# A two-block transformer on one core: GpSimd's weighing by a spread tensor, PE's first late sum moved, another order at the ends of two layers, a store in four parts

## The chip, the cores and the metric

The kernel runs on one core of one Trainium2 chip. The metric is the device time of one execution in microseconds (us). Engines are called PE (TensorE, matmuls), DVE (VectorE), ACT (ScalarE), POOL (GpSimd) and SP (SyncE, which only issues DMAs here).

## The reference

One sequence of 256 tokens with 1024 channels goes through two blocks of two layers each. All of it is in float32.

```python
def first_block(x, c, ...):
    for l in range(2):
        mod = silu(c) @ ada_w[l] + ada_b[l]
        sh_m, sc_m, gt_m, sh_f, sc_f, gt_f = split(mod, 6)
        h = rms_norm(x, norm_mix) * (1 + sc_m) + sh_m
        o_a, o_b, o_c = banded, sparse and delta mixers of split(h @ w_in)
        x = x + gt_m * (concat(o_a, o_b, o_c) @ w_out)
        h = rms_norm(x, norm_ffn) * (1 + sc_f) + sh_f
        gate, up = split(h @ w_gate_up)
        x = x + gt_f * ((silu(gate) * up) @ w_down)
    return rms_norm(x, final_norm)

def second_block(x, ...):
    for layer in range(2):
        h = rmsnorm(x, attn_norm[layer])
        mixed = 16 heads of biased attention on split(h @ w_in)   # even and odd layer differ
        x = x + mixed @ w_o[layer]
        h = rmsnorm(x, ffn_norm[layer])
        x = x + conv_ffn(h, w_up[layer], ..., w_down[layer])
    return rmsnorm(x, final_norm)
```

The change touches how a part of `silu(c) @ ada_w` is summed (a vector of 1024 times a matrix of 1024x512 for each of 24 chunks of the modulation), the order of work in `mixed @ w_o` of the even and the odd layer, and the store of the result.

## The kernel before, in words

Activations lie transposed: `x`, `h` and `mix` are [128 partitions, 8 channel tiles, 256 tokens]. Each weight matrix streams from memory in chunks of 512 columns into a ring of three slots. A float32 product is made of three PE matmuls of rounded operands (lines 655 to 657): every half chunk is copied in rounded form by ACT (`high`, line 1445, tile w_hi), DVE subtracts that from the original (`low`, line 1961, tile w_lo, two inputs in SBUF), and PE multiplies high by high, high by low and low by high. The order of every engine's work is written out by hand in the program; semaphores join them.

Phases that matter here, in order: layer 0 and layer 1 of the first block each end with "gu" (11 gate chunks of four output tiles, loop `up` on PE, three chunks for each turn of a loop) and "dn" (8 down tiles, `down` on PE). The second block has an even and an odd layer; each ends with attention woven into the output projection.

**The late modulation sums.** Of the 24 chunks of `silu(c) @ ada_w`, 16 are multiplied on PE. The 8 others, numbers 10 to 15 in layer 0 and 22 and 23 in layer 1, are loaded by POOL itself while gu and dn run, in two halves of 4 row tiles each (`load_half`). POOL multiplies each row tile of 128x512 by its column of silu(c) (line 2644), and adds the 8 products to one row of 512 (lines 2646, 2649, 2651, 2652); that is `weigh`. PE then sums the row over partitions with four small matmuls (`modulations`, line 772), for which it waits on POOL in its own order: behind gate chunk 3 (the first of them), behind gate chunk 9 (the second), and in layer 0's dn ahead of down tiles 2, 3, 5 and 7 (the table NEXT_ADA and `next_modulation`). `late_sums` has two rows, so POOL's first add of chunk m waits until PE has summed chunk m-2 (the wait on mod_ready):

```python
pool.wait_ge(mod_ready, m - 1)
ch(G.tensor_tensor(out, ada_late[:, 0, :], ada_late[:, 1, :], ALU.add))
```

**The ends of the even and the odd layer.** Eight attention units (u0 to u0+7) each pass scores (PE, line 787), `logits` (DVE, lines 1990 to 1993), `exps` (ACT, line 1476), `recip` (DVE, line 2006), probabilities (POOL, line 2622), `transposes` (PE, line 799), `copy_pt` (ACT, line 1487), `values` (PE, line 812) and `evac` (DVE, line 2018, into mix). `mix_high_woven` (ACT, line 1737) and `mix_low_woven` (DVE, line 1973) split finished tiles of mix, at tiles 0 to 3, 4 and 5, and 6 and 7 (mix_ready +1, +2, +3). The output projection is written as `out_part(l, half, k0, k1, tiles)`: the product of half chunk `half` over mix tiles k0 to k1, three matmuls for each k and output tile, into the PSUM banks of OUT_BANKS. PE runs it in pieces between the last units. `residual` (DVE, line 2303) then adds the finished tiles to x in order and makes w_lo of three further half chunks between them, before the next norm.

**The end.** `normalise_into` (DVE, line 1926) writes the 8 tiles of h, and SP stores all of h with one DMA behind the last (line 621).

## Time and profile before

| what | value |
|---|---|
| median of three runs | 1637.39 us (1636.44 to 1639.26) |
| the profiled execution, whole | 1637.26 us |
| its span, first to last instruction | 1635.0 us |
| PE busy | 1508.4 us, 92% |
| DVE, ACT, POOL busy | 60%, 50%, 20% |
| mean granted PE clock | 0.962 |

The profiled execution is 0.13 us below the median and 2.26 us longer than its span. A busy PE is not a PE at its peak: a matmul of 256 columns is reported with 0.28 us, while in a dense stretch one starts every 0.12 us. So the views by time are of more use than the busy share: what PE waits for, and what lies in order of time around those waits.

### The profile page before, as it was taken

What the parts mean: (1) busy time and instruction counts of PE and PEld (TensorE: products, weight loads), DVE (VectorE), ACT (ScalarE), POOL (GpSimd) and SP (SyncE); (2) the same over time, 40 slices, a digit from 0 to 9 for tenths busy, and PEclk for the clock granted to TensorE, in tenths of its full rate; (3) what the DMA queues carried; (4) which work ended last, traced back from release to release, by engine and by line L of the source; (5) the groups of instructions that cost most, each with busy time, mean ns of one, the idle gap of its engine ahead of it and who ended that gap; (6) DMA issues with size and microseconds to landing.
All of it is one profiled execution on the core that took longest, in us unless ns stands there. A gap on an engine that the chain in (4) does not pass through costs nothing.

```text
span 1635.0 us, 29653 instructions
## 1 busy us (share of the span) xinstructions
PE 1508.4 (92%) x12380; PEld 1436.1 (88%) x12380; DVE 975.5 (60%) x1342; ACT 810.9 (50%) x1319; POOL 323.5 (20%) x174
## 2 busy tenths in 40 slices
PE   6989978899979899888999998889999999799997
PEld 3988868899979888788999998879999998799997
DVE  2675446465446764574545658657785645577854
ACT  3764355343326643553434444546664555466642
POOL 0002202999850022039200000100000001000000
PEclk8999999899989999998999999999999999999999
DMA  9435745564642465254445642343544643334442
GB/s 388 170 143 233 255 162 199 193 252 178 253 173 98 152 242 197 79 206 177 184 152 184 221 155 104 112 165 142 200 154 161 226 155 115 143 128 182 172 153 88
DMA packets 31493, 287.91 MB, mean 176 GB/s; under 512 B 3032, under 2 KB 11512, under 8 KB 11929
## 3 DMA queue, kind: packets, MB, share of 16 engines
q1 hardware_dynamic: 26968, 267.42, 44.3%
q0 software_dynamic: 2304, 16.78, 2.7%
q10 hardware_dynamic: 2112, 2.15, 0.4%
q8 instruction: 84, 1.38, 0.3%
q14 instruction: 25, 0.20, 0.0%
HBM read 285.23 MB, written 7.39 MB: 179 GB/s over the span
## 4 chain that ended last, share of the span: by engine, by line
PE 71%; DVE 8%; POOL 8%; ACT 6%; DMA 3%; issue 3%; SPq 0%; DVEq 0%; POOLq 0%; ACTq 0%
PE bank L655 20%; PE bank L656 20%; PE bank L657 20%; POOL arena L2644 4%; ACT w_hi L1445 2%; DMA ring<-w_out 2%; DVE w_lo L1961 2%; PE bank L968 1%; PE bank L799 1%; PE bank L758 1%; PE bank L812 1%; POOL arena L2646 1%; DVE h L1926 1%; PE bank L772 1%; PE bank L734 1%
## 5 line engine op out<-in xcount | busy, mean ns | idle before, releaser
L655 PE MATMUL bank<-hi_T,w_hi 128*128 128x256 f32 x2184 | 633.9, 290 | 30.7 <-DVE h_lo L1946 17.0
L657 PE MATMUL bank<-hi_T,w_lo 128*128 128x256 f32 x2184 | 627.5, 287 | 0.0
L1961 DVE TENSOR_TENSOR w_lo<-ring,w_hi 128x2048 fp32r<-128x2048 f32 (+1 forms) x226 | 481.4, 2138 | 190.5 <-ACT w_hi L1445 188.8
L656 PE MATMUL bank<-h_lo,w_hi 128*128 128x256 f32 x2056 | 591.5, 288 | 0.0
L1445 ACT ACTIVATE w_hi<-ring 128x2048 fp32r<-128x2048 f32 (+1 forms) x226 | 391.8, 1735 | 275.0 <-PE bank L657 252.6
L655 PEld LDWEIGHTS bank<-hi_T,w_hi 128*128 128x128 f32 x2184 | 430.0, 197 | 36.7 <-issue 29.7
L657 PEld LDWEIGHTS bank<-hi_T,w_lo 128*128 128x128 f32 x2184 | 429.3, 197 | 0.0
L656 PEld LDWEIGHTS bank<-h_lo,w_hi 128*128 128x128 f32 x2056 | 405.2, 197 | 0.5 <-issue 0.2
L655 PE MATMUL bank<-act_hi,w_hi 128*128 128x256 f32 x704 | 200.7, 285 | 0.7 <-DVE w_lo L1961 0.7
L656 PE MATMUL bank<-act_lo,w_hi 128*128 128x256 f32 x704 | 200.0, 284 | 0.0
L657 PE MATMUL bank<-act_hi,w_lo 128*128 128x256 f32 x704 | 200.0, 284 | 0.0
L2644 POOL TENSOR_SCALAR arena<-arena,c_silu 128x512 f32<-128x512 f32 x64 | 146.0, 2294 | 9.3 <-DMA arena<-ada 8.6
L2622 POOL TENSOR_TENSOR arena<-arena,rec 128x512 f32<-128x512 f32 (+1 forms) x16 | 25.8, 1611 | 586.8 <-DVE rec L2006 586.8
L655 PEld LDWEIGHTS bank<-act_hi,w_hi 128*128 128x128 f32 x704 | 136.1, 193 | 1.2 <-DVE w_lo L1961 1.2
L656 PEld LDWEIGHTS bank<-act_lo,w_hi 128*128 128x128 f32 x704 | 136.0, 193 | 0.0
L657 PEld LDWEIGHTS bank<-act_hi,w_lo 128*128 128x128 f32 x704 | 136.0, 193 | 0.0
L2586 DVE SCALAR_TENSOR_TENSOR arena<-bank,v,arena 128x254 f32<-128x254 f32 (+1 forms) x176 | 72.7, 476 | 37.6 <-ACT arena L1897 37.4
L656 PE MATMUL bank<-mix_lo,w_hi 128*128 128x256 f32 x256 | 74.2, 290 | 0.0
L655 PE MATMUL bank<-w_hi,hi_T 128*128 128x256 f32 (+2 forms) x240 | 69.8, 291 | 0.0
L656 PE MATMUL bank<-w_lo,hi_T 128*128 128x256 f32 (+2 forms) x240 | 68.6, 286 | 0.0
L657 PE MATMUL bank<-w_hi,h_lo 128*128 128x256 f32 (+2 forms) x240 | 68.6, 286 | 0.0
L1897 ACT ACTIVATE arena<-bank,v 128x256 f32<-128x256 f32 x88 | 44.7, 558 | 43.6 <-PE bank L657 43.6
(270 smaller groups left out, 1963.8 us busy)
## 6 DMA issues: line engine op xcount, KB each, us to landing
ring<-w_gu SPq DMA_DIRECT2D x22, 2048.0 KB, 7.7
ring<-w_dn SPq DMA_DIRECT2D x32, 1408.0 KB, 6.1
ring<-w_up SPq DMA_DIRECT2D x22, 2048.0 KB, 7.9
ring<-ada SPq DMA_DIRECT2D x16, 2048.0 KB, 9.0
ring<-w_mix SPq DMA_DIRECT2D x11, 2048.0 KB, 8.3
arena<-ada POOLq DMA_DIRECT2D x16, 1024.0 KB, 7.2
ring<-even_in SPq DMA_DIRECT2D x8, 2048.0 KB, 7.7
ring<-odd_in SPq DMA_DIRECT2D x6, 2048.0 KB, 7.9
```

Source lines behind the costliest of these rows:

```text
L655: nc.tensor.matmul(out, wh, xh, start=start, stop=False)
L656: nc.tensor.matmul(out, wh, xl, start=False, stop=False)
L657: return nc.tensor.matmul(out, wl, xh, start=False, stop=stop)
L734: last = nc.tensor.matmul(bank[:, 7, 0:S], const("ones"), h[:, k, :], start=(k == 0), stop=(k == KT - 1))
L758: last = nc.tensor.matmul(bank[rows, 7, 0:S], c_wide[:, k, :], w[:, k, half * S:half * S + S], start=k < 4, stop=k >= 4, tile_position=(0, ...
L772: last = nc.tensor.matmul(bank[:, 7, at:at + 1], sums_m[:, t * P:t * P + P], ones, start=True, stop=True)
L1445: nc.scalar.activation(w_hi[:, u % AHEAD, 0:size], ring[:, slot, part * size:(part + 1) * size], ACT.Copy)\
L1897: last = nc.scalar.activation(cv[:, b, half, :], bank[:, 2 * b + half, 0:S], ACT.Identity, bias=cb[:, at], scale=cw[:, 2, at])
L1961: V.tensor_tensor(w_lo[:, n % SLOTS, at], ring[:, n % SLOTS, at], w_hi[:, u % AHEAD, 0:size].bitcast(F32), ALU.subtract).then_inc(w_lo_rea ...
L2586: V.scalar_tensor_tensor(out=cv[:, b, half, shift:S], in0=bank[:, 2 * b + half, 0:S - shift], scalar=cw[:, tap, at], in1=cv[:, b, half, sh ...
L2622: ins = G.tensor_tensor(out, out, along(rec[:, b, :], w), ALU.mult)
L2644: ch.mark(G.tensor_scalar(ada_late[:, k, :], ada_late[:, k, :], c_silu[:, k:k + 1], None, ALU.mult))
```

## The change

Six edits. (1) GpSimd's multiplications are written as a product of two tensors, the second being one column of c_silu spread over the 512 elements; the adds of 128x1024 are replaced by adds of 128x512, so that a half has three or four adds in a row, all of them behind the wait on mod_ready in the first half. (2) PE does the first late sum of each gu phase behind the sixth gate chunk instead of behind the third. (3) Even layer: on PE the product for output tile 3 moves ahead of the last transposes, and that for output tile 5 ahead of the wait for the last mix tiles, for which it gets PSUM bank 4 instead of 0; on DVE the second split of mix moves ahead of the last logits. (4) Odd layer: on PE the first product for output tile 2 moves ahead of `values(u0 + 5)`, and on DVE `evac(u0 + 4)` ahead of the last `recip`. (5) An explicit wait on logits_done in the even layer. (6) The result is stored by four DMAs of two tiles each.

```diff
--- before.py
+++ after.py
@@ -505,7 +505,7 @@
         stage("odd", biased_units(0, 2, 0, 4, 1, 0, False, 4), lg_odd)
 
         WOVEN = (0, 1, 7)
-        OUT_BANKS = (0, 1, 7, 2, 3, 0, 1, 2)
+        OUT_BANKS = (0, 1, 7, 2, 3, 4, 1, 2)
         MIXED_BANKS = (4, 5, 6, 0, 2, 3, 1, 4)
 
         def evacs_before(u):
@@ -617,9 +617,10 @@
             load_phase("o1", w_o2[1], 0, full)
             load_phase("up1", w_up2[1], 4, full)
             load_phase("down1", w_dn2[1], 2, FT * P)
-            sp.wait_ge(h_ready, norm_end[-1])
-            sp.dma_start(y, h[:, :, :]).then_inc(y_out, 16)
-            sp.wait_ge(y_out, 16)
+            for k in range(0, KT, 2):
+                sp.wait_ge(h_ready, norm_end[-1] - KT + k + 2)
+                sp.dma_start(y[:, k:k + 2, :], h[:, k:k + 2, :]).then_inc(y_out, 16)
+            sp.wait_ge(y_out, 16 * KT // 2)
 
 
         @block.tensor
@@ -1055,9 +1056,9 @@
                             one(j, i * (2 * SLOTS) + u0 + 2 * j + 1, i * (4 * SLOTS) + t0 + 4 * j - 3)
 
                 if m_next:
-                    turn(0, 1)
+                    turn(0, 2)
                     modulations(m_next - 1, m_next)
-                    turn(1, turns)
+                    turn(2, turns)
                 else:
                     turn(0, turns)
                 for j in range(SLOTS * turns, 11):
@@ -1294,15 +1295,16 @@
                 out_part(0, 0, 4, 6)
                 out_part(0, 1, 4, 6, (0,))
                 values(u0 + 6)
+                pe.wait_ge(logits_done, u0 + 8)
+                out_part(0, 1, 0, 6, (1,))
                 transposes(u0 + 7)
-                out_part(0, 1, 0, 6, (1,))
                 out_part(0, 2, 0, 6, (0,))
                 values(u0 + 7)
+                out_part(0, 2, 0, 6, (1,))
                 pe.wait_ge(mix_ready, mixed + 3)
                 out_part(0, 0, 6, KT)
                 out_part(0, 1, 6, KT)
-                out_part(0, 2, 6, KT, (0,))
-                out_part(0, 2, 0, KT, (1,))
+                out_part(0, 2, 6, KT)
                 out_part(0, 3, 0, KT)
 
             def odd_layer(first):
@@ -1359,9 +1361,9 @@
                 pe.wait_ge(mix_ready, mixed + 1)
                 out_part(1, 0, 0, 4)
                 values(u0 + 4)
+                out_part(1, 1, 0, 4, (0,))
                 values(u0 + 5)
                 transposes(u0 + 6)
-                out_part(1, 1, 0, 4, (0,))
                 pe.wait_ge(logits_done, u0 + 8)
                 out_part(1, 1, 0, 4, (1,))
                 values(u0 + 6)
@@ -2501,8 +2503,8 @@
                 logits(u0 + 6)
                 recip(u0 + 6)
                 evac(u0 + 5)
+                mix_low_woven(mixed + 2, slice(4, 6))
                 logits(u0 + 7)
-                mix_low_woven(mixed + 2, slice(4, 6))
                 recip(u0 + 7)
                 evac(u0 + 6)
                 evac(u0 + 7)
@@ -2552,8 +2554,8 @@
                 low(h0 + 11 + AHEAD)
                 logits(u0 + 7)
                 recip(u0 + 6)
+                evac(u0 + 4)
                 recip(u0 + 7)
-                evac(u0 + 4)
                 evac(u0 + 5)
                 mix_low_woven(mixed + 2, slice(4, 6))
                 evac(u0 + 6)
@@ -2641,15 +2643,18 @@
                 out = late_sums[:, m % 2, :]
                 pool.wait_ge(late_in[half], 16 * (ada_alone.index(m) + 1))
                 for k in range(k0, k0 + KT // 2):
-                    ch.mark(G.tensor_scalar(ada_late[:, k, :], ada_late[:, k, :], c_silu[:, k:k + 1], None, ALU.mult))
+                    ch.mark(G.tensor_tensor(ada_late[:, k:k + 1, :], ada_late[:, k:k + 1, :],
+                                            along(c_silu[:, k:k + 1], CH), ALU.mult))
                 ch.wait()
-                ch(G.tensor_tensor(ada_late[:, k0:k0 + 2], ada_late[:, k0:k0 + 2], ada_late[:, k0 + 2:k0 + 4], ALU.add))
                 if half == 0:
                     pool.wait_ge(mod_ready, m - 1)
                     ch(G.tensor_tensor(out, ada_late[:, 0, :], ada_late[:, 1, :], ALU.add))
-                else:
-                    ch(G.tensor_tensor(out, out, ada_late[:, k0, :], ALU.add))
-                    G.tensor_tensor(out, out, ada_late[:, k0 + 1, :], ALU.add).then_inc(acc_ready, 1)
+                for k in range(max(k0, 2), k0 + KT // 2):
+                    last = G.tensor_tensor(out, out, ada_late[:, k, :], ALU.add)
+                    if k < KT - 1:
+                        ch(last)
+                if half:
+                    last.then_inc(acc_ready, 1)
                     pool.wait_ge(acc_ready, m + 1)
                 if m_next is not None:
                     load_half(m_next, half)
```

GpSimd's row of instructions for one late chunk. Before, ada_late lies in arena and late_sums in pT:

```order
26 L2644 TENSOR_SCALAR arena<-arena,c_silu 128x512 x3
27 L2646 TENSOR_TENSOR arena<-arena 128x1024 [waits pool_chain]
28 L2649 TENSOR_TENSOR pT<-arena 128x512 [waits mod_ready,pool_chain]
29 L2635 DMA arena<-ada 128x2048 [waits pool_chain]
30 L2644 TENSOR_SCALAR arena<-arena,c_silu 128x512 [waits late_in1]
31 L2644 TENSOR_SCALAR arena<-arena,c_silu 128x512 x3
32 L2646 TENSOR_TENSOR arena<-arena 128x1024 [waits pool_chain]
33 L2651 TENSOR_TENSOR pT<-pT,arena 128x512 [waits pool_chain]
34 L2652 TENSOR_TENSOR pT<-pT,arena 128x512 [waits pool_chain]
35 L2635 DMA arena<-ada 128x2048 [waits acc_ready]
```

And the same stretch of the changed kernel:

```order
26 L2646 TENSOR_TENSOR arena<-arena,c_silu 128x512 x3
27 L2651 TENSOR_TENSOR pT<-arena 128x512 [waits mod_ready,pool_chain]
28 L2653 TENSOR_TENSOR pT<-pT,arena 128x512 [waits pool_chain] x2
29 L2637 DMA arena<-ada 128x2048 [waits pool_chain]
30 L2646 TENSOR_TENSOR arena<-arena,c_silu 128x512 [waits late_in1]
31 L2646 TENSOR_TENSOR arena<-arena,c_silu 128x512 x3
32 L2653 TENSOR_TENSOR pT<-pT,arena 128x512 [waits pool_chain] x4
33 L2637 DMA arena<-ada 128x2048 [waits acc_ready]
```

One add of 128x1024 stood ahead of the wait on mod_ready; now all three adds of the first half stand behind it.

DVE at the end of the even layer, before (L2018 is evac of unit 5, L1990 to L1993 the logits of unit 7, L1973 the second split of mix):

```order
713 L2018 COPY mix<-bank 128x2x128 [waits pv_done]
714 L1990 SCALAR_TENSOR_TENSOR arena<-bank,small,arena 128x1024 [waits trans_ready,scores_ready]
715 L1992 TENSOR_TENSOR arena<-arena 128x1024 [waits dve_chain]
716 L1993 TENSOR_REDUCE negm<-arena 128x4 [waits dve_chain]
717 L1973 TENSOR_TENSOR mix_lo<-mix,mix_hi_woven 128x512 [waits mix_hi_ready]
718 L2006 RECIPROCAL rec<-sums 128x4 [waits exps_done]
```

And changed:

```order
713 L2020 COPY mix<-bank 128x2x128 [waits pv_done]
714 L1975 TENSOR_TENSOR mix_lo<-mix,mix_hi_woven 128x512 [waits mix_hi_ready]
715 L1992 SCALAR_TENSOR_TENSOR arena<-bank,small,arena 128x1024 [waits trans_ready,scores_ready]
716 L1994 TENSOR_TENSOR arena<-arena 128x1024 [waits dve_chain]
717 L1995 TENSOR_REDUCE negm<-arena 128x4 [waits dve_chain]
718 L2008 RECIPROCAL rec<-sums 128x4 [waits exps_done]
```

The split now precedes the logits of unit 7 and waits for ACT's copy.

DVE at the end of the odd layer, before (the two L2006 are units 6 and 7, the two L2018 units 4 and 5):

```order
966 L1993 TENSOR_REDUCE negm<-arena 128x4 [waits dve_chain]
967 L2006 RECIPROCAL rec<-sums 128x4 [waits exps_done] x2
968 L2018 COPY mix<-bank 128x2x128 [waits pv_done] x2
969 L1973 TENSOR_TENSOR mix_lo<-mix,mix_hi_woven 128x512 [waits mix_hi_ready]
970 L2018 COPY mix<-bank 128x2x128 [waits pv_done] x2
```

And changed:

```order
966 L1995 TENSOR_REDUCE negm<-arena 128x4 [waits dve_chain]
967 L2008 RECIPROCAL rec<-sums 128x4 [waits exps_done]
968 L2020 COPY mix<-bank 128x2x128 [waits pv_done]
969 L2008 RECIPROCAL rec<-sums 128x4 [waits exps_done]
970 L2020 COPY mix<-bank 128x2x128 [waits pv_done]
971 L1975 TENSOR_TENSOR mix_lo<-mix,mix_hi_woven 128x512 [waits mix_hi_ready]
```

The evac of unit 4 no longer stands behind the reciprocal of unit 7.

## Rows read from the trace of the kernel before

**Rows 1.** The page: the chain that ended last, by engine.

```profile
PE 71%; DVE 8%; POOL 8%; ACT 6%; DMA 3%; issue 3%; SPq 0%; DVEq 0%; POOLq 0%; ACTq 0%
```

**Rows 2.** Waits of PE: us in total, times, longest.

```profile
PE bank L772 <- POOL pT L2652: 23.4, 3, 8.7
...
PE bank L655 <- DVE mix_lo L1973: 4.8, 2, 2.8
```

**Rows 3.** PE in order of time, three late sums: start, us, ..., [idle before <-releaser].

```profile
310.53 1.87 PE L772 MATMUL bank<-cn,pT 128*128 128x1 f32 x8 [7.38 <-POOL pT L2652]
...
382.97 0.95 PE L772 MATMUL bank<-cn,pT 128*128 128x1 f32 x8
...
473.79 1.87 PE L772 MATMUL bank<-cn,pT 128*128 128x1 f32 x8 [8.66 <-POOL pT L2652]
```

**Rows 4.** Windows: stretch, length, PE busy (x), PEld, DVE, ACT, POOL, PEclk, DMA.

```profile
475.00:479.00 4.00, 4.00 (x20) 4.00 (x20) 0.34 (x2) 0.00 (x0) 0.00 (x0) 0.50 0.00 0
480.00:484.00 4.00, 4.00 (x36) 4.00 (x35) 0.00 (x0) 1.92 (x1) 0.00 (x0) 1.00 0.00 0
```

**Rows 5.** Groups of POOL by form: xcount, busy us, mean ns, idle before.

```profile
L2644 POOL TENSOR_SCALAR arena<-arena,c_silu 128x512 f32<-128x512 f32 x64 | 146.0, 2294 | 9.3 <-DMA arena<-ada 8.6
...
L2622 POOL TENSOR_TENSOR lg<-lg,rec 128x512 f32<-128x512 f32 x6 | 6.2, 1040 | 51.8 <-DVE rec L2009 30.0 <-DVE rec L2006 21.8
L2664 POOL TENSOR_TENSOR arena<-arena,v 128x1024 f32<-128x1024 f32 x2 | 5.7, 2870 | 247.0 <-ACT arena L1470 247.0
```

**Rows 6.** The line L2644, min/median/max ns of its instructions.

```profile
L2644 POOL TENSOR_SCALAR arena<-arena,c_silu x64: 1552/1570/4327, 276.5 to 775.4; 128x512 f32<-128x512 f32 x64
```

**Rows 7.** POOL in order of time: a multiplication, an add, two adds of dn.

```profile
278.10 3.23 POOL L2644 TENSOR_SCALAR arena<-arena,c_silu 128x512 f32<-128x512 f32 x1
286.43 2.41 POOL L2646 TENSOR_TENSOR arena<-arena 128x1024 f32<-128x1024 f32 x1
...
423.82 2.28 POOL L2649 TENSOR_TENSOR pT<-arena 128x512 f32<-128x512 f32 x1 [5.58 <-PE bank L772]
...
440.58 1.30 POOL L2652 TENSOR_TENSOR pT<-pT,arena 128x512 f32<-128x512 f32 x1
```

**Rows 8.** DVE in order of time, w_lo beside those POOL instructions.

```profile
277.61 2.29 DVE L1961 TENSOR_TENSOR w_lo<-ring,w_hi 128x2048 fp32r<-128x2048 f32 x1 [1.15 <-ACT w_hi L1445]
282.10 2.29 DVE L1961 TENSOR_TENSOR w_lo<-ring,w_hi 128x2048 fp32r<-128x2048 f32 x1 [1.42 <-ACT w_hi L1445]
...
287.86 3.13 DVE L1961 TENSOR_TENSOR w_lo<-ring,w_hi 128x2048 fp32r<-128x2048 f32 x1 [1.42 <-ACT w_hi L1445]
```

**Rows 9.** DVE by form in 423.8 to 473.8 us (layer 0's dn).

```profile
L1961 DVE TENSOR_TENSOR w_lo<-ring,w_hi 128x1408 fp32r<-128x1408 f32 x11 | 20.6, 1906 | 1.2 <-ACT w_hi L1445 1.2
```

**Rows 10.** Even layer in order of time, three engines.

```profile
1074.83 0.57 ACT L1487 ACTIVATE pT<-bank 128x512 f32<-128x512 f32 x1
...
1086.25 0.38 PE L655 MATMUL bank<-mix_hi_woven,w_hi 128*128 128x256 f32 x1 [1.91 <-DVE mix_lo L1973]
...
1090.47 2.29 DVE L1961 TENSOR_TENSOR w_lo<-ring,w_hi 128x2048 fp32r<-128x2048 f32 x1 [1.52 <-ACT w_hi L1445]
...
1100.53 0.41 DVE L2303 TENSOR_TENSOR x<-x,bank 128x256 f32<-128x256 f32 x1
```

**Rows 11.** Odd layer in order of time, three engines.

```profile
1397.14 1.44 PE L812 MATMUL bank<-pT,arena 128*64 128x128 f32 x16 [3.49 <-DVE mix L2018]
...
1396.51 0.18 DVE L2006 RECIPROCAL rec<-sums 128x4 f32<-128x4 f32 x1 [2.06 <-ACT arena L1476]
...
1412.56 1.92 ACT L1445 ACTIVATE w_hi<-ring 128x2048 fp32r<-128x2048 f32 x1 [2.69 <-PE bank L657]
```

**Rows 12.** DVE's last tiles; two DMAs of SP: KB each, us to landing.

```profile
1627.45 3.25 DVE L1926 SCALAR_TENSOR_TENSOR h<-x,cn,rstd 128x256 f32<-128x256 f32 x8
...
y<-h SPq DMA_DIRECT2D x1, 1024.0 KB, 3.9
...
c_in<-c SPq DMA_DIRECT2D x1, 4.0 KB, 1.6
```

## The prediction

> **What bounds the kernel now.** I read the chain of waits first. It gives PE 71% and POOL 8% of the span [rows 1]. POOL's 8% is no gain to be had: the chain follows POOL's work backwards while PE has work of its own beside it. What PE loses is in the list of its waits: 23.4 us in three stalls on line 772, the late modulation sums, all on POOL's last add, and 4.8 us in two stalls on a split of mix [rows 2]. In order of time the three are 7.38 us at 303 to 310 us (layer 0, behind gate chunk 3), the same in layer 1 (23.4 less the other two leaves 7.4), and 8.66 us at 465 to 474 us, the last late sum of layer 0's dn [rows 3]. A stall costs more than its length: the granted clock in the 4 us behind the third is 0.50, the lower of its two levels (1.2 GHz), and 1.00 in the next window, with 20 matmuls against 36 [rows 4]. Sixteen matmuls at 0.12 us are about 1.8 us.
>
> **Edit 2, the first late sum three chunks later.** PE fell idle at 303.2 (310.53 less 7.38) and reached the second sum at 382.97 [rows 3], 79.8 us later. Between lie six gate chunks of 96 matmuls, 69.1 us at 0.12 us. The sum itself stays and takes 0.8 us, as it does unheld (the row at 382.97 shows 0.95). The rest, 9.9 us, goes: PE asks at about 338, and POOL was done at 310.5. Layer 1 has the same stall, so 19.8 us together. What waits for that sum is POOL's first add of chunk 12, which it reaches at about 347.
>
> **Edit 1, GpSimd.** How long the new multiplication takes is not in the trace. The old one takes 1.55 us when nothing holds it (minimum, and the median 1.57) and 2.29 in the mean [rows 5, 6]. The nearest row is the probabilities of the same engine, 128x512 times a column spread over 128 elements: 1.04 us in the mean of six. Another spread product, the scaling of z, took 2.87 for 128x1024, or 1.43 for 512 [rows 5]. I take 1.04 and keep 1.43 for the range, and 1.55 as the far end. Adds take 1.30 for 512 and 2.4 for 1024 [rows 7], so a half of four multiplications saves 2.0 and pays 0.3 for its adds.
>
> The Trainium skill speaks against this edit: its page GPSIMD Engine Reference, section 3.1, gives an op of two inputs 2.6 cycles for each element and one of a single input 1.03, so a product of two tensors would be 2.5 times as long as the one it replaces. By an estimate from its figure, 512 elements at 1.2 GHz are 1.1 us, which agrees with the 1.04 of the row; its figure for one input, 0.44 us, doesn't agree with the 1.55 measured, and the measurement decides.
>
> The difference of 2.29 and 1.55 is DVE. A multiplication that began at 278.10 while DVE made w_lo (277.61 to 279.9) took 3.23 us, and the w_lo at 287.86 took 3.13 instead of 2.29 beside POOL's add of 286.43 to 288.84. But the w_lo at 282.10 took its 2.29 beside a multiplication [rows 7, 8]. So an instruction of two tensors on either engine holds up the other, and the old multiplication is held up without holding. The new one both is held and holds. I replayed layer 0 by this rule, with DVE's starts from the trace. With the old instructions it ends at 473.3, where the trace has 473.8 (the 473.79 of rows 3).
>
> Now the third stall. From the release by PE at 423.8 (where POOL had idled 5.58) [rows 7] POOL takes 50 us to 473.8: 12 multiplications at 1.55, three adds at 2.4, six at 1.3, two DMA issues at 0.95 and gaps, 36.3 us, and so 13.6 us held up. New: 12 at 1.04 and 14 adds at 1.30 (also the 2.4 us that stood ahead of the wait now stand behind it), with the rest 34.0 us. DVE makes 12 w_lo of about 1.6 us in that time [rows 9] (eleven, and the last of the size before them), 19.2 us. If these hold POOL up as much as before, the piece is 2.3 us shorter; if fully, 3.3 longer. The replay gives 50.4, so **0.5 us longer**. POOL must also come in time to that release, now about 413.8. By the replay it does, with 5.8 us to spare; at 1.30 for a multiplication it comes 7.3 late. What DVE loses is at most 1.3 us a w_lo. In gu that is nothing to PE, which has 5.8 us of matmuls in each half chunk and its w_lo two of them ahead. In dn the first w_lo of a pair has the 4.0 us (33 matmuls) of one half: 0.8 for the add before it, at most 1.3 held and 1.6 of its own are 3.7, just inside.
>
> **Edit 4, odd layer.** PE stalls 3.49 us on evac, which stood behind the reciprocal of unit 7 at 1396.51; without it, it can run at about 1394.5. From PE's idle at 1393.65 to ACT's next copy at 1412.56 [rows 11], which waits for the first two finished output tiles, are 18.9 us. The work between is 78 matmuls at 0.12 (9.4) and five groups of transposes and values (4.3) with 0.2 of latency: 13.9. Behind the move of 12 matmuls nothing else is late: POOL's last probabilities end at 1398.7, where PE arrives at 1398.7. So **5.0 us** go, which is the stall and 1.6 of the clock. Low end 3.5, the stall alone.
>
> **Edits 3 and 5, even layer.** The split comes about 2.9 us earlier and its stall goes. But unit 7's logits start 1.5 us later, and ACT copies unit 6's transposes (1074.83) only behind unit 7's exponentials. It does so at 1076.3 now, and PE, which reaches `values(u0 + 6)` at 1072.9, stalls there 3.9 us. Behind it the reordered work fills the second stall of 1.91: PE begins the last mix tiles at about 1087.3, against 1086.25 at half clock. ACT's copy behind the first two output tiles, and with it the next w_lo, come 0.2 later than 1090.47. From there DVE has no gap until its last add at 1100.53 [rows 10], so that PE's earlier end, some 3 us, helps nobody. **0.2 us longer**; ends: 1.5 either way. The new wait on logits_done is met by 1074.3.
>
> **Edit 6, the store.** 1024 KB land 3.9 us behind the issue, 4 KB 1.6 [rows 12]. The tiles come every 0.4 us, so three quarters are on their way before the last pair is done. What is left is 1.6 and a quarter of 2.3, 2.2: **1.7 us** go. Ends: nothing, and three quarters of 3.9, 2.9.
>
> **Sum.** 1637.26 - 19.8 + 0.5 - 5.0 + 0.2 - 1.7 = **1611.5 us** against the profiled execution, which is 0.13 below the median of the runs.
>
> **The rivals.** *Layer 0's gain is given back in dn.* POOL's sums are one chain from 276 to 474 us. At 1.30 us for a multiplication the replay ends 17.0 us behind PE instead of 8.7: 8.3 back instead of 0.5, 1619.3. At 1.43 it is some 5 us more, 1624. For it: the scaling of z. Against: six rows of 1.04. Chance 0.14.
>
> *More than the sum.* The hold-up stays as it was (2.8 us less than forecast), and the even layer gets PE's 3 us because DVE finds its copies earlier: 1611.5 - 5.8 = 1606. Against: DVE's chain without a gap. Chance 0.14.
>
> *Slower.* If a product of two tensors is longer than the one it replaces, the last late sum in dn0 decides. The replay ends 25.9 us behind PE at 1.55 and 35 us later for each further microsecond, so from about 1.9 us all is lost: 25.9 + 12.4 = 38.3, less 8.7, are 29.6 against the 26.5 gained elsewhere, 1640. At 2.5 times 1.55 it would be 3.9 us and over 1700. The page's rule named above would bring this. No row has it. Chance 0.03.
>
> *The stall only moves.* PE could wait as long behind chunk 6. It would need POOL at 338 instead of 310; excluded by the rows, unless the price is that of the slower case.
>
> **Chances.** Forecast 0.67 (1608 to 1615), given back 0.14, more 0.14, slower 0.03, and 0.02 that these cancel. The range from 1605 to 1620 holds the first three but for their ends. A measurement of this kernel tells 0.2%, 3.3 us, from no change. Faster 0.95, same 0.02, slower 0.03.
>
> **What the profile would show.** Right: two waits on line 773 (the old 772) gone, the third at 9 us; the multiplication at 1.04 when unheld; w_lo beside it longer than 2.29; a stall of some 4 us on ACT's copy in the even layer, and its last DVE add no earlier than now against the start of the layer; no stall on evac in the odd layer; 2.2 us from last issue to landing. A third stall of over 12 us, or one behind chunk 6, would make the prediction wrong.

## The result and the profile after the change

The changed kernel takes **1610.93 us** (median of 4 runs, 1609.76 to 1612.69) against 1637.39 before (4 runs, 1636.44 to 1639.26): a ratio of 0.9838, 95% interval 0.9821 to 0.9855, which is 26.5 us less. The forecast was 1611.5, with 1605 to 1620. The profiled execution took 1609.89 us with a span of 1608.1.

The changed kernel, page: busy time by engine, and the chain that ended last. In the changed kernel PE's lines are one higher than before, those of the other engines two.

```profile
PE 1499.7 (93%) x12380; PEld 1428.8 (89%) x12380; DVE 1008.6 (63%) x1342; ACT 811.0 (50%) x1319; POOL 293.6 (18%) x190
...
PE 76%; DVE 7%; ACT 6%; POOL 4%; DMA 3%; issue 3%; SPq 0%; DVEq 0%; ACTq 0%; POOLq 0%
```

PE's share of the chain went from 71 to 76% and POOL's from 8 to 4% [rows 1]. The changed kernel, waits of PE (us in total, times, longest):

```profile
PE bank L773 <- POOL pT L2653: 6.5, 1, 6.5
PE bank L813 <- ACT pT L1489: 6.2, 3, 3.9
...
PE bank L656 <- DVE w_lo L1963: 3.3, 4, 1.5
PE bank L735 <- DVE h L2325: 3.2, 2, 1.8
```

Three stalls of 23.4 us on the late sums have become one of 6.5, and both waits on a split of mix [rows 2] are gone. New is a stall of 3.9 us on ScalarE's copy of transposes. The waits on w_lo, 1.1 us in all before, are 3.3, and those on the norm's h 3.2 instead of 1.8. In order of time (start, us, [idle before <-releaser]):

```profile
336.15 0.95 PE L773 MATMUL bank<-cn,pT 128*128 128x1 f32 x8
...
371.59 0.95 PE L773 MATMUL bank<-cn,pT 128*128 128x1 f32 x8
...
400.74 0.39 PE L656 MATMUL bank<-act_hi,w_hi 128*128 128x256 f32 x1 [1.11 <-DVE w_lo L1963]
...
461.95 1.86 PE L773 MATMUL bank<-cn,pT 128*128 128x1 f32 x8 [6.50 <-POOL pT L2653]
```

The first sum no longer waits. The last one, 473.79 with 8.66 of idle before [rows 3], waits 6.50. Behind it the clock falls as it did [rows 4]; the changed kernel, windows with PEclk third from the end:

```profile
463.00:467.00 4.00, 4.00 (x19) 4.00 (x20) 0.34 (x2) 0.00 (x0) 0.00 (x0) 0.50 0.00 0
```

POOL, by group and by line (min/median/max ns):

```profile
L2653 POOL TENSOR_TENSOR pT<-pT,arena 128x512 f32<-128x512 f32 x48 | 103.0, 2146 | 3.8
L2646 POOL TENSOR_TENSOR arena<-arena,c_silu 128x512 f32<-128x512 f32 x64 | 85.7, 1367 | 9.1 <-DMA arena<-ada 8.7
```

```profile
L2646 POOL TENSOR_TENSOR arena<-arena,c_silu x64: 1029/1036/3087, 275.0 to 761.9; 128x512 f32<-128x512 f32 x64
```

A multiplication takes 1.04 us unheld, as forecast, and 1.37 in the mean, where it was 1.57 and 2.29 [rows 5, 6]. The Trainium skill (GPSIMD Engine Reference, section 3.1) would have the product of two tensors cost 2.5 times the one-input form. An estimate from its two-input figure is 1.1 us and agrees with the 1.04; one from its one-input figure, 0.44, does not agree with the 1.57, and so its rule, as applied to these two forms, fell.

**The ledger.** Profiled execution against profiled execution, measured between the same PE or DVE instructions:

| stretch | edit | forecast | measured |
|---|---|---|---|
| start to gate chunk 0 of layer 0 | none | 0 | -1.5 |
| to the second late sum | 2 | -9.9 | -9.9 |
| to the last late sum of dn | 1 | +0.5 | -0.5 |
| gate of layer 1 | 2 | -9.9 | -9.8 |
| even layer up to its end | none | 0 | -1.7 |
| even layer's end | 3, 5 | +0.2 | +1.7 |
| odd layer's end | 4 | -5.0 | -4.9 |
| last tile to end of span | 6 | -1.7 | -1.4 |
| the rest, three stretches | none | 0 | +1.1 |
| outside the span | none | 0 | -0.5 |

The sum is -27.4, the 1637.26 less 1609.89 of the two executions. The lines without an edit come to -2.6 together.

### The profile page after: what moved, and what is told of

Same layout as the page of the kernel before. It is cut to its first block, busy times and chain, and to the rows that moved or that the text cites. A ratio compares the mean times of both kernels' runs of the same rounds, so it can differ in the third digit from the quotient of the medians.

```text
span 1608.1 us, 29671 instructions
## 1 busy us (share of the span) xinstructions
PE 1499.7 (93%) x12380; PEld 1428.8 (89%) x12380; DVE 1008.6 (63%) x1342; ACT 811.0 (50%) x1319; POOL 293.6 (18%) x190
## 3 DMA queue, kind: packets, MB, share of 16 engines
q8 instruction: 84, 1.38, 0.3%
## 4 chain that ended last, share of the span: by engine, by line
PE 76%; DVE 7%; ACT 6%; POOL 4%; DMA 3%; issue 3%; SPq 0%; DVEq 0%; ACTq 0%; POOLq 0%
PE bank L656 22%; PE bank L657 21%; PE bank L658 21%; ACT w_hi L1447 2%; DMA ring<-w_out 2%; DVE w_lo L1963 2%; POOL pT L2653 2%; PE bank L969 1%; DMA ring<-ada 1%; PE bank L800 1%; PE bank L759 1%; PE bank L813 1%; POOL arena L2646 1%; PE bank L967 1%; PE bank L952 1%
## 5 line engine op out<-in xcount | busy, mean ns | idle before, releaser
L1963 DVE TENSOR_TENSOR w_lo<-ring,w_hi 128x2048 fp32r<-128x2048 f32 (+1 forms) x226 | 506.0, 2246 | 180.0 <-ACT w_hi L1447 178.2
L2653 POOL TENSOR_TENSOR pT<-pT,arena 128x512 f32<-128x512 f32 x48 | 103.0, 2146 | 3.8
L2646 POOL TENSOR_TENSOR arena<-arena,c_silu 128x512 f32<-128x512 f32 x64 | 85.7, 1367 | 9.1 <-DMA arena<-ada 8.7
```

The lines of the kernel that those rows point to most:

```text
L1963: V.tensor_tensor(w_lo[:, n % SLOTS, at], ring[:, n % SLOTS, at], w_hi[:, u % AHEAD, 0:size].bitcast(F32), ALU.subtract).then_inc(w_lo_rea ...
L2646: ch.mark(G.tensor_tensor(ada_late[:, k:k + 1, :], ada_late[:, k:k + 1, :], along(c_silu[:, k:k + 1], CH), ALU.mult))
L2653: last = G.tensor_tensor(out, out, ada_late[:, k, :], ALU.add)
```

## The experiments

Each kernel's time stands beside runs of the kernel before on the same chip, in the same session (medians 1637.16 for the first four, 1635.76 for the next four, 1636.61 for the last four). Differences of one or two microseconds are at the limit of these timings. "Less" is the difference of the medians. The ratio is not taken from the medians and can read up to 1.6 us more or less than they do. The changed kernel was timed in a session of its own, in which the kernel before took 1637.39. So a difference to it goes across sessions: read by the ratios, the earlier sum of chunk 12 below is worth 5.2 us and not 8.1, ScalarE's other order 2.0 and not 3.5, and chaining alone costs 2.0. Against the chained kernel, timed beside them, the first two are worth 7.8 and 3.2. Where this matters, the stretches of the traces decide.

### One edit at a time

The first three take one part of the change alone; GpSimd's edit is whole in the second.

```diff
-                    turn(0, 1)
+                    turn(0, 2)
                     modulations(m_next - 1, m_next)
```

> The kernel before with edit 2 alone (first late sum behind gate chunk 6). Theory (GpSimd's chain bounds dn of layer 0): the two stalls of 7.4 us go, 19.8 us with their clock, but GpSimd no longer gets a pause of DVE at 303 to 310 us, and by the replay with the old instructions it ends at 468.5 where PE arrives at 455.1: the stall at the last late sum of layer 0 grows from 8.7 to 13.4 us. Together 15 us less, about 1622. Rival (the last stall has nothing to do with the first): it stays 8.7 us, and the time falls by the full 19.8 us to about 1617.5.

Measured: 1623.04 us, ratio 0.9915 (0.9902 to 0.9928), 14.1 less (13.9 by the ratio). The kernel with edit 2 alone, PE in order of time:

```profile
441.38 1.43 PE L772 MATMUL bank<-cn,pT 128*128 128x1 f32 x8 [3.51 <-POOL pT L2652]
...
469.86 1.87 PE L772 MATMUL bank<-cn,pT 128*128 128x1 f32 x8 [8.47 <-POOL pT L2652]
```

Both 7.4 us stalls are gone, but a new one appears ahead of the sum of chunk 14, and the last stays: 12.0 us in two, where the theory had 13.4 in one. Of edit 2's 19.8 us about 5.7 are given back in dn when GpSimd keeps its old instructions; in the trace the last sum stands 97.4 us behind the second (372.43 to 469.86), where it was 90.8. The rival, by which the last stall has nothing to do with the first, fell.

```diff
-                    ch.mark(G.tensor_scalar(ada_late[:, k, :], ada_late[:, k, :], c_silu[:, k:k + 1], None, ALU.mult))
+                    ch.mark(G.tensor_tensor(ada_late[:, k:k + 1, :], ada_late[:, k:k + 1, :],
+                                            along(c_silu[:, k:k + 1], CH), ALU.mult))
...
```

> The kernel before with edit 1 alone (GpSimd's products of two tensors, adds of 512). Theory (GpSimd is faster by what it no longer is held up, since products without a wait between them keep DVE out for the whole group of four): the sums of chunks 10 and 22 are ready 5 us earlier, so the first stalls of the two layers fall from 7.4 to about 2.3 us each, the last one of layer 0 from 8.7 to about 6.5, and w_lo beside a group of products takes up to 6.7 us. 12 to 16 us less, 1621 to 1625. Rival (the forecast's replay, in which DVE gets in behind every product): the first stalls fall by 1.4 us only, the last grows by 0.5: 3 us less, 1634.

Measured: 1624.72, ratio 0.9931 (0.9918 to 0.9943), 12.4 less (11.3 by the ratio). The kernel with edit 1 alone:

```profile
303.61 1.87 PE L772 MATMUL bank<-cn,pT 128*128 128x1 f32 x8 [2.80 <-POOL pT L2651]
...
466.86 1.87 PE L772 MATMUL bank<-cn,pT 128*128 128x1 f32 x8 [6.50 <-POOL pT L2651]
...
745.78 1.05 PE L772 MATMUL bank<-cn,pT 128*128 128x1 f32 x8 [1.44 <-POOL pT L2651]
```

The first stall shrinks from 7.38 to 2.80, layer 1's from as much to 1.44, and the last of layer 0 from 8.66 to 6.50. That is what the theory had, and the rival's 1634 fell. Most of what edit 1 gains alone is in the two stalls that edit 2 removes as well, so the two can't be added up.

```diff
+                out_part(1, 1, 0, 4, (0,))
                 values(u0 + 5)
                 transposes(u0 + 6)
-                out_part(1, 1, 0, 4, (0,))
...
                 recip(u0 + 6)
+                evac(u0 + 4)
                 recip(u0 + 7)
-                evac(u0 + 4)
```

> The kernel before with edit 4 alone (odd layer: product for tile 2 ahead of values of unit 5, evac of unit 4 ahead of the last reciprocal). Theory: 4.9 us less, as between the two traces, 1632.4; no stall on evac. Rival (what the stretch gained came with the shifted clock): under 3.5 us, the stall alone.

Measured: 1632.51, ratio 0.9965 (0.9952 to 0.9977), 4.7 less (5.7 by the ratio). The stall on evac is gone from PE's waits. The theory had 4.9.

The even layer's edits alone:

> The kernel before with the even layer's edits alone (3 and 5). Theory: 1.7 us slower than before, 1639: a stall of 3.9 us on ACT's copy of unit 6's transposes takes the place of two stalls of 2.8 and 1.9, DVE's last add comes 0.7 us later against the start of the stretch, and the norm's sums on PE run at the lower clock because PE idles ahead of them (1.0 us). Rival (the 1.7 us are a phase of the clock): between 1 us faster and 0.5 slower. The profile's stretch from the first product with mix to the first matmul of the next phase tells them apart: 44.9 against 43.2 us before.

Measured: 1636.31, or 1635.50 without the one of its twelve executions that took 3661.44; ratio, without that one, 0.9993 (0.9984 to 1.0002). The time does not bear out a loss. The trace does in part: from the first mix product to the start of the next phase are 43.9 us, where it was 43.2 and 44.9 was expected, with the foreseen 3.9 us stall in it. What the edits cost was left open here.

```diff
-            sp.wait_ge(h_ready, norm_end[-1])
-            sp.dma_start(y, h[:, :, :]).then_inc(y_out, 16)
+            for k in range(0, KT, 2):
+                sp.wait_ge(h_ready, norm_end[-1] - KT + k + 2)
+                sp.dma_start(y[:, k:k + 2, :], h[:, k:k + 2, :]).then_inc(y_out, 16)
```

> The kernel before with the store cut in four alone. Forecast of the prediction: 1.7 us less. The stretch from DVE's last tile of the result to the end of the span measured 4.30 us before and 2.86 us after the change; the theory is that this stretch is 2.9 us here too, since nothing of the layer ahead of it plays a part, so 1.4 less, 1636. The rival: four stores take longer each (2.5 us to landing beside 3.9 for the one), and SP's issues of them, one every 0.7 us, set the end: then the stretch stays above 3.5 us and the time within 0.8 us of before.

Measured: 1634.14, ratio 0.9993 (0.9984 to 1.0002); the timing alone doesn't tell 1.6 us from nothing. The span of 1633.9 ends 2.9 us behind DVE's last tile, which ends at 1631.0 there, so the stretch is as the theory has it. The changed kernel has the same: DVE's last tiles, and SP's stores (KB each, us to landing).

```profile
1601.98 3.26 DVE L1928 SCALAR_TENSOR_TENSOR h<-x,cn,rstd 128x256 f32<-128x256 f32 x8
```

```profile
y<-h SPq DMA_DIRECT2D x4, 256.0 KB, 2.5
```

From 1605.2 to 1608.1 are 2.9 us, against 4.3 before. A store of a quarter takes 2.5 us in the median instead of 3.9 [rows 12].

### Does GpSimd's group of multiplications keep DVE out?

In the changed kernel PE waits 1.1 us for w_lo at the start of dn: the w_lo at 397.19, of 128x1408, took 3.50 us where one alone takes 1.6. Before that DVE falls behind. The changed kernel, POOL and then DVE in order of time:

```profile
346.11 4.03 POOL L2646 TENSOR_TENSOR arena<-arena,c_silu 128x512 f32<-128x512 f32 x4
350.22 11.57 POOL L2653 TENSOR_TENSOR pT<-pT,arena 128x512 f32<-128x512 f32 x4
...
362.70 4.03 POOL L2646 TENSOR_TENSOR arena<-arena,c_silu 128x512 f32<-128x512 f32 x4
```

```profile
346.21 6.09 DVE L1963 TENSOR_TENSOR w_lo<-ring,w_hi 128x2048 fp32r<-128x2048 f32 x1 [1.16 <-ACT w_hi L1447]
...
362.22 6.66 DVE L1963 TENSOR_TENSOR w_lo<-ring,w_hi 128x2048 fp32r<-128x2048 f32 x1 [1.26 <-ACT w_hi L1447]
```

A w_lo that takes 2.29 us alone [rows 8] takes 6.09 beside four multiplications that run in 4.03 with nothing between them: 4.03 and 2.29 are 6.3. Not every group does this. The same trace, the first group of layer 0 and the w_lo beside it:

```profile
275.02 6.09 POOL L2646 TENSOR_TENSOR arena<-arena,c_silu 128x512 f32<-128x512 f32 x4 [4.32 <-DMA arena<-ada]
```

```profile
276.21 2.99 DVE L1963 TENSOR_TENSOR w_lo<-ring,w_hi 128x2048 fp32r<-128x2048 f32 x1 [1.16 <-ACT w_hi L1447]
```

Here DVE got in: the group's third multiplication took 3.08 us, the others 1.03 or 1.04. Of the 16 groups six run in 4.03, with a w_lo that ends only 1.5 or 2.2 us behind the group (its own time or a little less); in six others DVE gets in before the end, and in the other four the first multiplication waits for a w_lo that is already on. The edit puts a wait between the multiplications:

```diff
-                    ch.mark(G.tensor_tensor(ada_late[:, k:k + 1, :], ada_late[:, k:k + 1, :],
-                                            along(c_silu[:, k:k + 1], CH), ALU.mult))
-                ch.wait()
+                    ch(G.tensor_tensor(ada_late[:, k:k + 1, :], ada_late[:, k:k + 1, :],
+                                       along(c_silu[:, k:k + 1], CH), ALU.mult))
```

> The changed kernel, with each of GpSimd's four multiplications of a half waiting for the one before it. Theory: with nothing between them the four keep DVE out for all their 4.03 us, which is why two w_lo beside them took 6.09 and 6.66 us and PE waits 1.1 us for a w_lo at the start of dn. With a wait between them DVE gets in: the longest w_lo of layer 0 is below 4 us, and that 1.1 us stall is gone. GpSimd pays for it: it is held up by DVE more often, and the third stall grows from 6.5 us to some 8 or 9. In sum within 2 us of the changed kernel, 1610 to 1613. The rival: DVE is kept out by something else (the length of its own queue of work, or the adds), the longest w_lo stays at 6 us or more and the stall on it stays.

Measured: 1610.59, ratio 0.985 (0.9836 to 0.9863), the changed kernel's time within the noise. The chained kernel: DVE's w_lo in layer 0 (min/median/max ns), POOL's multiplications beside them, and PE's last late sum.

```profile
L1963 DVE TENSOR_TENSOR w_lo<-ring,w_hi x38: 1615/2460/3375, 268.5 to 474.1; 128x2048 fp32r<-128x2048 f32 x22, 128x1408 fp32r<-128x1408 f32 x16
```

```profile
346.90 7.90 POOL L2646 TENSOR_TENSOR arena<-arena,c_silu 128x512 f32<-128x512 f32 x4
```

```profile
462.03 1.86 PE L773 MATMUL bank<-cn,pT 128*128 128x1 f32 x8 [8.81 <-POOL pT L2652]
```

The longest w_lo falls from 6.66 to 3.38 us, the stall on w_lo in dn is gone, and the four multiplications of this group take 7.90 instead of 4.03. The last sum runs at 462.03 as against 461.95: what PE gains ahead of it, it waits for GpSimd. So the theory held in each place, and it shows why the time doesn't move: GpSimd's chain to that sum sets the end of dn, not DVE.

### Where does the last stall hang?

```diff
+                next_modulation(1)
                 pe.wait_ge(hidden_ready, done)
                 part_sum(0, 1)
                 part_sum(1, 1)
-                next_modulation(1)
```

> The changed kernel; in dn of layer 0 PE does the late sum of chunk 12 at the start of dn, ahead of its wait for the hidden half, and not behind the first output tile. Theory: the last stall (6.5 us on GpSimd's last add, and 1.8 us of lower clock behind it) hangs on the release of GpSimd by that sum, which comes some 8 to 9 us earlier; the replay then has GpSimd done at 451 to 453 us, ahead of PE at 455. Stall gone: 8 us less than the changed kernel, 1602.5 to 1604. The rival: GpSimd isn't done with chunk 12 when PE asks for it there, and PE waits at the start of dn for what it gains at the end (no change); or the last sum is set by the loads of GpSimd's chunks, and the stall stays above 3 us.

Measured: 1602.82, ratio 0.9806 (0.9792 to 0.9819), 8.1 less than the changed kernel. In the traces the spans differ by 8.2 us. Of that 6.2 lie in dn, between the matmuls at 404.80 and 468.08 us of the changed kernel; the rest lies in stretches without an edit. With the earlier sum, PE in order of time:

```profile
403.53 0.95 PE L773 MATMUL bank<-cn,pT 128*128 128x1 f32 x8
...
458.11 0.94 PE L773 MATMUL bank<-cn,pT 128*128 128x1 f32 x8
```

and its waits between 380 and 465 us:

```profile
PE bank L656 <- DVE w_lo L1963: 3.8, 2, 2.7
```

The stall is gone: POOL's last add ends at 449.3 us, the sum runs at 458.1. What stands out now are the w_lo stalls, 3.8 us, so chaining should be worth something here. The w_lo behind the longer one, 2.7, is this; it began 0.46 us behind a group that took 4.03:

```profile
410.05 5.07 DVE L1963 TENSOR_TENSOR w_lo<-ring,w_hi 128x1408 fp32r<-128x1408 f32 x1 [0.99 <-ACT w_hi L1447]
```

(The expectation below names 5.73 for it; that is a w_lo of gu, at 379.11.)

> The changed kernel with the late sum of chunk 12 at the start of dn, and GpSimd's multiplications chained. With the earlier sum alone PE still waits 3.8 us for two w_lo in dn (2.7 and 1.1 us), one of which DVE made in 5.73 us and one in 3.50 instead of 2.29 and 1.6, and the clock falls behind it. Theory: chaining takes these two stalls away (the longest w_lo below 4 us), GpSimd's last sum comes some 2 us later than with the earlier sum alone but still ahead of PE, and the two together are worth more than apart: 3 to 6 us less than the 1602.8 of the earlier sum alone, 1597 to 1600. The rival: GpSimd, held up more, comes behind PE again by 2 us or more, and the time stays at 1602 to 1604, as chaining alone brought nothing.

Measured: 1598.70, ratio 0.9763 (0.9749 to 0.9778), 4.1 less again. Both stalls on w_lo are gone; POOL ends at 452.8 and the last sum runs without a wait:

```profile
454.45 0.95 PE L773 MATMUL bank<-cn,pT 128*128 128x1 f32 x8
```

The same edit brought nothing while GpSimd's chain set the end, and 4 us once it didn't.

### What the even layer's edits cost

The changed kernel at the layer's end: PE, then ACT, then DVE.

```profile
1054.05 0.66 PE L813 MATMUL bank<-pT,arena 128*64 128x128 f32 x8 [3.88 <-ACT pT L1489]
```

```profile
1053.42 0.57 ACT L1489 ACTIVATE pT<-bank 128x512 f32<-128x512 f32 x1
```

```profile
1078.46 0.41 DVE L2305 TENSOR_TENSOR x<-x,bank 128x256 f32<-128x256 f32 x1
...
1081.66 1.75 DVE L1924 RECIPROCAL rstd<-std 128x256 f32<-128x256 f32 x1 [2.79 <-ACT std L1417]
```

ACT's copy stands behind the exponentials of unit 7, which themselves wait for the later logits. The first experiment moves the copy ahead of them:

```diff
+                out_part(0, 2, 0, 6, (0,))
                 transposes(u0 + 7)
-                out_part(0, 2, 0, 6, (0,))
...
+                copy_pt(u0 + 6)
                 exps(u0 + 7)
-                copy_pt(u0 + 6)
```

> The changed kernel; in the even layer ScalarE copies the transposes of unit 6 ahead of the exponentials of unit 7, and PE does the first piece of the third output tile ahead of the transposes of unit 7. Theory: the 3.9 us stall on ScalarE's copy was made by the order on ScalarE and goes; PE comes to the last mix tiles some 3 us earlier, and half of it or more reaches the norm since PE's matmuls run at the higher clock: 1607.5 to 1609.5. The rival, from the prediction: DVE's chain without a gap up to its last add sets the end of this stretch, and the time stays within 0.5 us of the changed kernel, 1610.5 to 1611.5, with the wait ahead of the norm's sums longer by as much as the stall was.

Measured: 1607.42, ratio 0.9826 (0.9812 to 0.9839), 3.5 less than the changed kernel. Its reciprocal of the norm:

```profile
1079.40 1.75 DVE L1924 RECIPROCAL rstd<-std 128x256 f32<-128x256 f32 x1 [2.74 <-ACT std L1417]
```

From the first mix product (1041.57 there, 1040.34 in the changed kernel) these are 37.8 us against 41.3. DVE's chain moved up by the whole 3.5: the rival, by which it sets the end whatever PE does, fell.

> The changed kernel without its edits in the even layer. The even edits alone gave 1.1 us less, with an interval of 1.5 either way, while the stretch in the trace was 0.7 us longer alone and 1.7 us longer in the changed kernel. Theory: they cost 0.7 to 1.7 here, and without them it is 1609.2 to 1610.2. The rival: they are worth 1 us or more, as the first timing has it, and without them it is 1612 or above.

Measured: 1607.05, ratio 0.9816 (0.9802 to 0.9831), 3.9 less than the changed kernel. Both the theory's range and the rival fell: the even edits cost more than forecast. The stretch below shows 2.2 of it; the rest of the 3.9 lies where the two kernels are the same, and between sessions. Without them:

```profile
1079.22 1.75 DVE L1923 RECIPROCAL rstd<-std 128x256 f32<-128x256 f32 x1 [1.83 <-ACT std L1416]
```

The same stretch (from 1040.15) is 39.1 us here, 41.3 with them, 39.6 in the kernel before (1063.13 to 1102.77) and 40.4 in the kernel with the even edits alone (1060.85 to 1101.21). So the same edit costs 0.7 in the one setting and 2.2 in the other. Of the difference, 0.6 is that the kernel before, with the same instructions as this one, was itself slower there: its 102 matmuls behind the second stall start over 13.7 us, in this kernel over 12.2, of which 0.9 is won back by a shorter wait for h ahead of the norm's sums (0.43 us instead of 1.38). The other 0.9 is in the norm's sums. The changed kernel, and then the even edits alone:

```profile
1078.60 2.52 PE L735 MATMUL bank<-h,cn 128*128 128x256 f32 x6 [1.83 <-DVE h L2325]
```

```profile
1099.10 1.56 PE L734 MATMUL bank<-h,cn 128*128 128x256 f32 x6 [1.83 <-DVE h L2324]
```

After the same stalls (1.5 on w_lo, 1.8 on h) six matmuls take 2.52 us in the one and 1.56 in the other. Windows over them, first of the changed kernel, then of the even edits alone, with PEclk third from the end:

```profile
1078.60:1081.10 2.50, 2.50 (x6) 1.51 (x6) 0.27 (x1) 0.42 (x1) 0.00 (x0) 0.59 0.87 347
```

```profile
1099.10:1100.70 1.60, 1.56 (x6) 1.05 (x6) 0.28 (x1) 0.42 (x2) 0.00 (x0) 1.00 0.78 307
```

The granted clock fell in the changed kernel (0.59), and not in the other. With ScalarE's other order the six took 2.47, again behind the same two stalls. What decides whether the clock falls behind a short stall was not settled.

All three edits together, on top of the change:

> All three edits on top of the change: the earlier sum of chunk 12, the chained multiplications, and ScalarE's and PE's other order at the end of the even layer. Theory: the last is in another stage and adds its 3.5 us: 3 to 4 us less than the run with the first two, 1593.5 to 1596.5. The rival: by the phase of the clock part of it is lost, 1 to 2 us less only.

Measured: 1596.96, ratio 0.9748 (0.9728 to 0.9767), with runs from 1591.16 to 1598.08. It is the fastest kernel here, 14.0 below the changed one and 39.7 below the runs of the kernel before beside it, and half a microsecond above the range of the theory. The third edit's own share is unclear in these timings: 1.7 by the medians, at the rival's value, where the trace has the stretch from 170.6 to 167.2 us between the reciprocals of the norms around the even layer's body, the 3.5 of the theory. One comparison of medians this close doesn't decide it.

### What GpSimd's edit is worth beside the others

> The changed kernel with GpSimd's old instructions (a multiplication by a column, and a 128x1024 add per half). GpSimd's edit alone gave 11.3 us, most of it from the stalls that the later first sum takes away too. Theory: on top of the other edits it is worth only what its stalls in dn of layer 0 show: 12.0 us in two without it, 6.5 and 1.1 us with it, and one fall of the clock of 1.8 us, 6.2 in sum, so 1617. The rival: it is worth its whole 11.3 us, 1622; or, by the prediction's own replay, which had the last stall no shorter with it, nothing: 1611.

Measured: 1617.31, ratio 0.9882 (0.9864 to 0.9900), 6.4 more than the changed kernel. The changed kernel with the old GpSimd instructions, waits of PE:

```profile
PE bank L773 <- POOL pT L2654: 12.0, 2, 8.5
```

12.0 us in two stalls as against 6.5 and 1.1, and one more fall of the clock: the forecast 6.2 held. It is neither the 12.4 of the edit alone nor nothing.

## Why the prediction was right, step by step

**Edit 2, 9.9 us in each layer.** Right to 0.1 us: PE's idle start to the second sum, less the matmuls and the sum that stay, was the whole account, since GpSimd had long been done.

**Edit 1, the price.** 1.04 us was taken from the probabilities on the same engine, and 1.036 is the median. The row nearest in form was the right one; the scaling of z, at 1.43 for 512, was not.

**Edit 1, "the replay gives 50.4, so 0.5 us longer".** This term failed, in sign: from PE's release at 413.8 POOL takes 48.1 us, not 50.4, which is 1.8 less than before. Ahead of it PE lost 1.4 that it had not lost before, 1.1 of them to the stall on w_lo, so that the stretch is 0.5 shorter in all. The replay took each multiplication as holding DVE and being held in turn. With a wait between them, in the chained kernel, that is so, and POOL takes 50.1 us from its release to its last add (411.90 to 461.98), near the replay's 50.4. In the changed kernel the groups of four behind the release took 4.03, 4.47 and 6.80 us; beside the first two DVE came in only at the end, beside the third before it. In the chained kernel they took 7.11, 6.94 and 6.92. So GpSimd gained by the groups, though not by each. The release, in the changed kernel and then in the chained one:

```profile
413.81 2.28 POOL L2651 TENSOR_TENSOR pT<-arena 128x512 f32<-128x512 f32 x1 [14.62 <-PE bank L773]
```

```profile
411.90 2.29 POOL L2650 TENSOR_TENSOR pT<-arena 128x512 f32<-128x512 f32 x1 [10.89 <-PE bank L773]
```

"What DVE loses is at most 1.3 us a w_lo" failed with it: DVE lost up to 4.4 (6.66 less 2.29), and the margin of the first w_lo in dn, called "just inside", was not: it took 3.50 where 2.9 was allowed, and PE stalled 1.1. That GpSimd would come in time to the release held, by 14.6 us of idle where 5.8 were forecast.

**What edit 1 does.** The prediction priced it only as an addition to edit 2 and never asked what edit 2 would bring without it. The runs answer: 14.1 instead of 19.8. So edit 1, priced as a loss of 0.5, is worth 6.4 beside the others.

**Edit 4.** 5.0 forecast, 4.9 in the ledger, 4.7 in the run alone (5.7 by the ratio).

**Edits 3 and 5, +0.2.** The stall on ScalarE's copy came as worked out, 3.9 forecast and 3.88 in the trace. The step that failed is the one behind it: the layer's end. PE gains less than the stalls that go, then waits 1.5 us for w_lo and 1.8 for h, since DVE has the same work to do, and the norm's sums start on a lower clock. That is 1.7 in the ledger, the upper end of the bound given, and 2.2 against the same kernel without these edits, beyond it. Of the 1.7 the lower clock in the norm's sums is 1.0 (2.52 us instead of 1.56, which they took in the kernel before too); the other 0.7 is what the edits cost alone. "DVE has no gap until its last add" was true as a row, but it did not fix the end: with ScalarE's copy moved, the whole chain came 3.5 us earlier.

**Edit 6.** 1.7 forecast, 1.4 measured: the last pair takes 2.9 us from the last tile to the end of the span. The four stores' median of 2.5 to landing stands where 2.2 was estimated. That this is the store's doing rests on that stretch in the traces, not on the timing.

**The 2.6 us nobody forecast.** The stretches without an edit vary. The reciprocals of the first two norms of DVE, around attention in layer 0, in the kernel before and in the kernel with all three edits, where neither the change nor the edits touch a thing:

```profile
24.44 1.75 DVE L1922 RECIPROCAL rstd<-std 128x256 f32<-128x256 f32 x1 [23.55 <-ACT std L1415]
...
262.43 1.75 DVE L1922 RECIPROCAL rstd<-std 128x256 f32<-128x256 f32 x1 [1.75 <-ACT std L1415]
```

```profile
24.93 1.75 DVE L1924 RECIPROCAL rstd<-std 128x256 f32<-128x256 f32 x1 [24.02 <-ACT std L1417]
...
259.65 1.75 DVE L1924 RECIPROCAL rstd<-std 128x256 f32<-128x256 f32 x1 [1.75 <-ACT std L1417]
```

238.0 us in the one and 234.7 in the other; the kernel with the earlier sum and the chain has 238.3. A term below 3 us can be read in its own stretch of a trace, but not off two whole times. So the forecast of 1611.5 owes some of its closeness to terms that cancelled: +1.0 on the last sum and -1.5 on the even layer, and 2.6 that were in no term.

## What to carry to other kernels

When a kernel has a chain of gated work beside its main engine, price an edit that removes an early stall together with what the gated engine then does with its earlier release: here a later sum gave back 5.7 of 19.8 us until GpSimd's work became shorter, and moving one other release forward by a few lines was worth 6 to 8 more. An edit that takes waits out of a stretch whose end another chain sets, like the chained multiplications, brings nothing until the wait that ends last is gone; try it again then. And where a copy stands behind other work on its engine, reorder that engine too, or the reordering on PE only moves the stall.

## What was not expected of the hardware

A group of GpSimd's two-tensor multiplications with nothing between them can keep DVE's two-tensor operations out until the group's end: 4.03 us of multiplications beside w_lo of 6.09 and 6.66 us, instead of 2.29. It did so in six of the changed kernel's 16 groups; in six others DVE got in before the end, as beside the group of 6.09 us at 275.02. What decides between the two was not found. With a wait between the multiplications the longest w_lo of layer 0 is 3.38, and none of the 16 groups runs in less than 6.00. The multiplication by a column, on the other hand, let the w_lo at 282.10 take its 2.29 [rows 8]. The Trainium skill (SBUF — State Buffer, "Who interferes with whom") says that a DVE instruction with two SBUF inputs contends with a GpSimd instruction that reads SBUF, and that the first to issue has the ports for the whole instruction while the other blocks. For the two-tensor form the trace agrees that one keeps the other out. It doesn't agree that the one instruction that issues first holds: in the six groups it was the whole group, and the w_lo at 362.22 began 0.48 us ahead of its group and was the one held. For the form with a column, which reads SBUF too, it doesn't agree: DVE wasn't held beside it.

The even layer's end showed the other thing: after the same two short stalls, six matmuls took 2.52 us in one kernel and 1.56 in another.
